# Two-layer encoder trunk on one Trainium2 core: other places for the short steps of seven-product pairs, and one weight sum moved from VectorE to an adding DMA

## What is computed

```python
h = rms_norm(x, mixer_norm_w)
# layer 0: q,k,v,u,g = split(h @ w_in); windowed attention beside gMLP gating
# layer 1: q,k,v = h @ w_qkv; stick-breaking attention
x = x + mixed @ w_out
h = rms_norm(x, ffn_norm_w)
x = x + (silu(h @ w_gate) * (h @ w_up)) @ w_down     # hidden width 5632
```

## Time and profile before

| | before |
|---|---|
| median of 3 runs | 2050.72 us (2050.27 to 2052.87) |
| the profiled execution | 2051.17 us, span 2049.4 us |
| PE busy | 2033.7 us, 99% |
| DVE busy | 1661.7 us, 81% |
| ACT busy | 1087.5 us, 53% |
| POOL busy | 162.7 us, 8% |
| DMA, mean | 221 GB/s |
| steps, matmuls of them | 846, 8724 |

### The profile page before, as it was taken

How to read it: one execution, slowest core, us unless ns; L and a number is a source line. 1 busy time by engine, 2 the same in 40 slices (tenths; PEclk the granted TensorE clock), 3 DMA queues, 4 the chain that set the end, 5 groups by cost and what they waited for, 6 DMA issues and landing times.

```text
span 2049.4 us, 23323 instructions
## 1 busy us (share of the span) xinstructions
PE 2033.7 (99%) x9176; PEld 1675.6 (82%) x9176; DVE 1661.7 (81%) x1859; ACT 1087.5 (53%) x1250; POOL 162.7 (8%) x271
## 2 busy tenths in 40 slices
PE   9999999999999999999999999999999999999999
PEld 8878878888888888888888888878888888888887
DVE  7777898888788887887666777888888788887986
ACT  6565555555445554555555455555554455544453
POOL 1010110010001000011111110110100001000010
PEclk9999999999999999999999999999999999999999
DMA  9665666566665666668767877676566666666664
GB/s 329 216 216 184 219 228 231 200 216 226 207 225 199 216 222 219 211 205 271 248 211 245 266 236 214 219 239 212 205 219 219 220 205 206 232 220 210 208 210 174
DMA packets 216431, 453.72 MB, mean 221 GB/s; under 512 B 10545, under 2 KB 10561, under 8 KB 216065
## 3 DMA queue, kind: packets, MB, share of 16 engines
q1 hardware_dynamic: 197600, 392.72, 56.1%
q0 software_dynamic: 18304, 57.37, 9.3%
q10 hardware_dynamic: 416, 2.13, 0.3%
HBM read 422.82 MB, written 29.36 MB: 221 GB/s over the span
## 4 chain that ended last, share of the span: by engine, by line
PE 60%; issue 29%; DMA 7%; DVE 2%; POOL 2%; ACT 0%; SPq 0%; POOLq 0%; DVEq 0%
PE acc L1483 17%; PE acc L1489 17%; PE acc L1484 17%; DMA spread<-blocks 3%; DMA blocks<-folded 3%; POOL spread L643 2%; PE turn_zb L1531 1%; PE turn_zb L1528 1%; PE turn_zb L1527 1%; PE acc L1531 1%; PE acc L1528 1%; PE acc L1527 1%; DVE w_lo L970 1%; DMA raw<-in_w_in 1%; DVE tsum L990 0%
## 5 line engine op out<-in xcount | busy, mean ns | idle before, releaser
L717 ACT ACTIVATE w_hi<-raw 128x1024 fp32r<-128x1024 f32 x710 | 742.4, 1056 | 494.5 <-PE acc L1489 479.2
L970 DVE TENSOR_TENSOR w_lo<-raw,w_hi 128x1024 fp32r<-128x1024 f32 x710 | 854.2, 1220 | 157.3 <-ACT w_hi L717 154.8
L1483 PE MATMUL acc<-w_hi,xT_hi 128*128 128x512 f32 x1664 | 649.9, 391 | 0.7 <-ACT w_hi L717 0.7
L1484 PE MATMUL acc<-w_hi,xT_lo 128*128 128x512 f32 x1664 | 647.7, 389 | 0.0
L1489 PE MATMUL acc<-w_lo,xT_hi 128*128 128x512 f32 x1664 | 444.9, 389 | 0.0
L1483 PEld LDWEIGHTS acc<-w_hi,xT_hi 128*128 128x128 f32 x1664 | 312.3, 188 | 67.9 <-issue 1.3
L1489 PEld LDWEIGHTS acc<-w_lo,xT_hi 128*128 128x128 f32 x1664 | 312.3, 188 | 65.1
L1484 PEld LDWEIGHTS acc<-w_hi,xT_lo 128*128 128x128 f32 x1664 | 312.4, 188 | 64.7
L717 ACT ACTIVATE w_hi<-tsum 128x1024 fp32r<-128x1024 f32 x136 | 144.5, 1062 | 303.0 <-DVE tsum L990 286.5
L1483 PE MATMUL acc<-w_hi,m_hi 128*128 128x512 f32 x764 | 297.9, 390 | 0.0
L1484 PE MATMUL acc<-w_hi,m_lo 128*128 128x512 f32 x764 | 297.3, 389 | 0.0
(11 more groups left out here) (222 smaller groups left out, 1676.8 us busy)
## 6 DMA issues: line engine op xcount, KB each, us to landing
raw<-in_w_gate SPq DMA_DIRECT2D x88, 1024.0 KB, 5.3
raw<-in_w_up SPq DMA_DIRECT2D x88, 1024.0 KB, 5.2
raw<-in_w_down SPq DMA_DIRECT2D x88, 1024.0 KB, 5.3
raw<-in_w_qkv SPq DMA_DIRECT2D x48, 1024.0 KB, 6.7
raw<-in_w_out SPq DMA_DIRECT2D x32, 1024.0 KB, 5.2
raw<-in_w_in SPq DMA_DIRECT2D x26, 1024.0 KB, 6.4
blocks<-folded POOLq DMA_DIRECT2D x42, 512.0 KB, 3.2
spread<-blocks POOLq DMA_DIRECT2D x168, 128.0 KB, 2.9
```

Source lines behind the costliest of these rows:

```text
L717: nc.scalar.activation(w_hi[:, h.slot, :, :], source(h), ACTF.Copy).then_inc(hi_ready, 1)
L970: nc.vector.tensor_tensor(w_lo[:, h.slot, :, :], source(h), f32(w_hi[:, h.slot, :, :]), ALU.subtract).then_inc(lo_ready, 1)
L1483: nc.tensor.matmul(dst, hi[:, h.k0 + k, at], wh, start=h.opens and k == 0, stop=False)
L1484: nc.tensor.matmul(dst, lo[:, h.k0 + k, at], wh, start=False, stop=False)
```

## The change

1. **Opening.** The order becomes A4 A6 B4 B6 A8 A10 B8 B10, then the seven short steps (outer P corner R outer Q W), then A12 A14 B12 B14. P, R and W are made ahead of steps 8, 10 and 13. The units are loaded in the new order.
2. **12-tile pairs.** A4 A6 B4 B6, then the seven short steps, then A8 A10 B8 B10.
3. **All other pairs.** The order is A4 A6 outer P B4 corner B6 R A8 Q outer W, and then as before. P, R and W are made ahead of steps 2, 6 and 10.
4. **Q's sum.** DVE no longer makes it. POOL issues a transfer from SBUF to SBUF, `raw[even] += raw[odd]` on chunk b's first unit (512 KB are added to 512 KB), as soon as the pair's P is made. ACT waits `q_added` before it rounds Q's weights, which it now reads from `raw`. That slot stays taken until Q's `w_lo` is made. POOL issues it between bounces, by step numbers (`FOLD_AT`).
5. **Wide corrections.** Pairs of VectorE instructions on 512 columns become one on 1024: the last two of `corrections`, the two of `corrected`, and the two that read PSUM in `leave` of gate and of up. A wide one waits for both row halves.

The core of the diff:

```diff
-SUMS = "PQRW"
-SUM_AT = {2: "P", 4: "Q", 7: "R", 10: "W"}
+SUMS = "PRW"
+SUM_AT = {2: "P", 6: "R", 10: "W"}
...
-    front = [A(4), A(6), ("outer", a, 0), ("P", -1, 0), B(4), ("Q", -1, 0), B(6), ("corner", b, 0), ("R", -1, 0)]
+    front = [A(4), A(6), ("outer", a, 0), ("P", -1, 0), B(4), ("corner", b, 0), B(6), ("R", -1, 0), A(8), ("Q", -1, 0), ("outer", a, 2), ("W", a, 0)]
     sums = dict(SUM_AT)
+    short = [("outer", a, 0), ("P", -1, 0), ("corner", b, 0), ("R", -1, 0), ("outer", a, 2), ("Q", -1, 0), ("W", a, 0)]
     if order == "opening":
-        sums = {2: "P", 4: "Q", 7: "R", 9: "W"}
-        steps = (front[:6] + [B(6), ("corner", b, 0), ("R", -1, 0), ("outer", a, 2), ("W", a, 0), A(8), A(10), B(8), B(10), A(12), A(14), B(12), B(14)])
-        units = [(a, 4), (b, 0), (a, 0), (b, 4), (a, 8), (b, 8), (a, 12), (b, 12)]
+        sums = {8: "P", 10: "R", 13: "W"}
+        steps = [A(4), A(6), B(4), B(6), A(8), A(10), B(8), B(10)] + short + [A(12), A(14), B(12), B(14)]
+        units = [(a, 4), (b, 4), (a, 8), (b, 8), (a, 0), (b, 0), (a, 12), (b, 12)]
     elif order == "together" and tiles == 12:
-        sums = {2: "P", 4: "Q", 7: "R", 9: "W"}
-        steps = front + [("outer", a, 2), ("W", a, 0), A(8), A(10), B(8), B(10)]
-        units = [(a, 4), (b, 0), (a, 0), (b, 4), (a, 8), (b, 8)]
+        sums = {4: "P", 6: "R", 9: "W"}
+        steps = [A(4), A(6), B(4), B(6)] + short + [A(8), A(10), B(8), B(10)]
+        units = [(a, 4), (b, 4), (a, 0), (b, 0), (a, 8), (b, 8)]
...
+            def add_q(pair):
+
+                slot = pair.it.unit_of(pair.b, 0) % RING
+                pool.wait_ge(sum_made, len(SUMS) * pair.n + 1)
+                pool.dma_start(raw[:, slot, 0::2, :], raw[:, slot, 1::2, :], accum_op=ALU.add).then_inc(q_added, 16)
...
             for F in range(len(FOLDS)):
                 if F == qk0 + 8:
                     bounce_weights(3)
+                for pair in PAIRS:
+                    if (FOLD_AT[F - 1] if F else 0) < pair.q_sum_at <= FOLD_AT[F]:
+                        add_q(pair)
                 bounce(F)
...
+                elif h.kind == "Q":
+                    act.wait_ge(q_added, 16 * h.pair.n + 16)
...
-                nc.vector.tensor_tensor(corr[:, 2, :], product[5], corr[:, 2, :], ALU.subtract)
-                nc.vector.tensor_tensor(corr[:, 3, :], product[5], corr[:, 1, :], ALU.subtract).then_inc(corr_made, 1)
+                nc.vector.tensor_tensor(corr[:, 2:4, :], product[5].unsqueeze(1).to_broadcast([P, TT, CH]), corr[:, 2:0:-1, :],
+                                        ALU.subtract).then_inc(corr_made, 1)
```

More of the change, by code:

```diff
@@ L108, in __init__ @@
         self.steps, self.units, sums = seven_steps(a, a + 1, tiles, order)
+        self.q_sum_at = it.base + first + min(sums)
         self.sums = {first + s: form for s, form in sums.items()}
@@ L166, in __init__ @@
         self.unit0 = unit0
-        self.halves = [Half(base + s, s, c, k, self.unit_of(of[s].a if c < 0 else c, k), kind, of[s]) for s, (kind, c, k) in enumerate(steps)]
+        homes = [c if c >= 0 else of[s].b if kind == "Q" else of[s].a for s, (kind, c, k) in enumerate(steps)]
+        self.halves = [Half(base + s, s, c, k, self.unit_of(homes[s], k), kind, of[s]) for s, (kind, c, k) in enumerate(steps)]
         for c in range(ph.chunks):
@@ L188, in release @@
         if k == 0 and self.pair_of(c):
-            last = max(last, max(t for t, form in self.pair_of(c).sums.items() if form in ("PQR" if c % 2 else "PW")))
+            last = max(last, max(t for t, form in self.pair_of(c).sums.items() if form in ("PR" if c % 2 else "PW")))
+            if c % 2:
+                last = max(last, max(h.s for h in self.halves if h.kind == "Q" and h.pair is self.pair_of(c)))
         return self.base + last
@@ L276, with group_start @@
             for c in ([1] if it.ph.name == "up" else range(2) if it.ph.name == "qkv" else range(it.ph.chunks))])
+GROUP0 = 22
+def group_start(g):
+    return GROUP0 + 7 * g
+FOLD_AT = ([group_start(g) + 6 + AHEAD for g in range(A_KV)]
+           + [it.base + it.fold_at(c) + AHEAD for it in ITERATIONS if it.ph.folds and it.ph.n
+              for c in ([1] if it.ph.name == "up" else [c for c in range(3) if QKV[it.i][c][0] != "v"] if it.ph.name == "qkv" else range(it.ph.chunks))])
 def splits(F):
@@ L514, in source @@
             if h.kind in SUMS:
-                return tsum[:, int(h.kind == "Q"), :, :]
+                return tsum[:, 0, :, :]
+            if h.kind == "Q":
+                return raw[:, h.raw_slot, 0::2, :]
             if h.kind == "corner":
@@ L669, in _ @@
                     bounce_weights(weights_follow[F])
+            for pair in PAIRS:
+                if pair.q_sum_at > FOLD_AT[-1]:
+                    add_q(pair)
             base = 2 * (D // CH) * (RESIDUALS - 1)
@@ L981, in weight_sum @@
                     out_to, a, b = tsum[:, 0, :, :], raw[:, gate % RING, even, :], first
[L982 to L983 removed]
                 elif form == "R":
[L985 removed]
+                    dve.wait_ge(sum_made, len(SUMS) * n + 1)
                     out_to, a, b = tsum[:, 0, :, :], tsum[:, 0, :, :], second
                 else:
[L988 removed]
+                    dve.wait_ge(sum_made, len(SUMS) * n + 2)
                     out_to, a, b = tsum[:, 0, :, :], tsum[:, 0, :, :], raw[:, gate % RING, odd, :]
@@ L1058, in corrected @@
                 dve.wait_ge(corr_made, pair.n + 1)
-                for tt in range(TT):
-                    xs = x_sb[:, tt, c * CH:(c + 1) * CH]
-                    nc.vector.tensor_tensor(xs, xs, corr[:, 2 * (c % 2) + tt, :], ALU.add).then_inc(x_corrected, 1)
+                xs = x_sb[:, :, c * CH:(c + 1) * CH]
+                nc.vector.tensor_tensor(xs, xs, corr[:, 2 * (c % 2):2 * (c % 2) + TT, :], ALU.add).then_inc(x_corrected, TT)
             def evacuate(it, c, dst, const=None):
@@ L1147, in leave @@
                     if c == 0:
-                        for tt in range(TT):
-                            dve.wait_ge(products_done, 2 * it.last_half(0) + tt + 1)
-                            nc.vector.tensor_tensor(hid[:, tt, :], acc[:, it.pair(0), tt, :], corr[:, tt, :], ALU.add).then_inc(acc_read, 1)
+                        dve.wait_ge(products_done, 2 * it.last_half(0) + TT)
+                        nc.vector.tensor_tensor(hid[:, :, :], acc[:, it.pair(0), :, :], corr[:, 0:TT, :], ALU.add).then_inc(acc_read, TT)
                         return
-                    for tt in range(TT):
-                        dve.wait_ge(products_done, 2 * it.last_half(1) + tt + 1)
-                        nc.vector.tensor_tensor(corr[:, 2 + tt, :], acc[:, it.pair(1), tt, :], corr[:, 2 + tt, :], ALU.add).then_inc(acc_read, 1)
+                    dve.wait_ge(products_done, 2 * it.last_half(1) + TT)
+                    nc.vector.tensor_tensor(corr[:, TT:, :], acc[:, it.pair(1), :, :], corr[:, TT:, :], ALU.add).then_inc(acc_read, TT)
                     dve.wait_ge(silu_done, ph.up0 + i + 1)
```

14 lines of the change are left out of this document (4 added, 10 removed).

## The result

The changed kernel takes **2063.17 us**, median of 4 runs (2061.86 to 2063.89), against 2051.28 us for the kernel before in the same session (4 runs, 2050.27 to 2052.87). The ratio is 1.0056, 95% interval 1.0042 to 1.0070: slower, by 11.9 us where 4.1 were forecast. The profiled execution took 2063.52 us, span 2061.7 us, 12.3 us longer than the span before.

A forecast was written before the change was run, and what follows sets the result against it. PE, busy 99% of the span, was taken as the bound. Openings +0.3, 12-tile pairs +2.3 and clock +1.5 gave +4.1 us, from 2050.7 to 2054.8 us; own range 2051 to 2060, wide range 2046 to 2064.

The forecast's parts named there:

- The gap at A8: In the openings: PE stands still 5.5 us at A8, now step 4, until chunk 2 of the stationary operand is ready.
- the two sums that leave: In the opening: DVE no longer makes sums P and Q before `var`, so the chain to `xT_lo` moves forward 2.27 us.
- rival 2: Openings win: chunk 2 comes sooner, PE waits 1.9 us at A8, -3.4 us per opening, total 2042.6; chance 0.16.
- Q in the openings: At Q in each opening: DVE's `w_lo` comes 0.5 us after PE wants it.
- The clock: PE's clock may fall to half speed after the openings' gaps; at most 3.0 us lost per opening, +1.5 taken.
- an even chance for each gap: The clock falls or holds with even chance in each opening's gap; 1.5 us was charged once.
- rival 4: Both clocks fall in full in the openings: +0.3 + 2.3 + 6.0, total 2059.3; no separate chance, within the forecast's range.
- The adding transfer: POOL's transfer for Q's sum takes 5.25 us, with 3.5 as lower and 11.0 as upper bound.
- The 12-tile pairs: Waits at A8 (0.77 us) and B8 (1.15), together 1.9 against 0.78 before: +1.15 each, +2.3 in all.
- The other 30 pairs: Outside openings and 12-tile pairs: transfer and saved DVE work hidden behind PE, costed at nothing.
- 1 (the clock holds): Rival, all even: the clock holds and the transfer takes 3.5 to 5 us, total 2049.7 to 2052.5; chance 0.22.
- 3 (a transfer over 9 us): Rival, slow adding transfer: +8 to +14 us at the 12-tile pairs, 2072 us at an 11 us transfer; chance 0.12.

The follow-up runs named there:

- early2: The changed kernel with chunk 2 of the stationary operand taken on ACT and DVE three steps earlier in the output phase: 2045.99 us, ratio 0.9968.
- fill2: The changed kernel with 24 warm-up products on PE ahead of its wait for chunk 2 at A8 in both openings: 2060.73 us, ratio 1.0045.
- dve_q: The changed kernel with Q's sum back on DVE and no adding transfer, new orders and wide corrections kept: 2059.25 us, ratio 1.0040.
- narrow: The changed kernel with all wide corrections split again into 512-column instructions: 2062.39 us, ratio 1.0047.
- before_early: The kernel before the change with only chunk 2 taken three steps earlier: 2052.28 us, ratio 1.0005.

## Why the prediction was right, and where it was not

The verdict (slower, with 2063.17 inside 2046 to 2064) was right, the forecast time 8.4 us too low. The measured time lies above the forecast's own range, 2051 to 2060, and 0.8 us from the edge of the wide one, and the loss is nearly three times the +4.1 that was added up. That sum lay on the line between no change and slower, with 0.45 against 0.40, so there was some luck in the verdict; what made it come out clear is that every term of the sum was larger than forecast. The places where PE would wait were right. By its steps:

- **The gap at A8**, 5.5 us: 5.74 and, in the second opening, 5.92. The reckoning by the two sums that leave (2.27 us; 2.28 measured) held. What it said of the cause was wrong in one word: the chain doesn't *hang on* the norm's scale. Chunk 2 only stood behind it in program order, as early2 shows, and rival 2 ("chunk 2 comes sooner") was one edit away; its gap of 1.9 us and its -3.4 per opening were too cautious, since early2 has no gap and -5.3.
- **Q in the openings**, 0.5 us late: 0.53 in both. With the gaps the orders alone gave 5.74 + 5.92 + 2 x 0.53 = 12.7 us where 2 x 5.84 = 11.7 were lost before: +1.0, and +0.3 was forecast.
- **The clock**, +1.5 us: the term that was mis-sized. It fell in both gaps, and in each PE was already at work for 5.57 and 3.99 us of the low stretch, half of which is lost: 2.8 + 2.0 = **4.8 us**; fill2, without it, gives 4.9 (2.4 in each, so the sums agree better than the openings one by one). The step that failed is "an even chance for each gap" and half of the loss; rival 4's price of 3.0 each was nearer. An even chance in each of two gaps at 3.0 us would have been 3.0, and the prediction gives no reason for taking half of that, with the warm-up rows showing half speed after idling. The Trainium skill's rule ("TensorE: Matmul & The Clock Gate", What's actually happening), that the throttled state is the default and activity lifts it, charged both gaps, +3.0 as I had written it. The trace agrees with it: the clock fell in both gaps, at a price of 4.8 us and not 3.0.
- **The adding transfer**, 5.25 us: 5.33 in the 12-tile pair, 5.1 median to landing over 34. In the two openings it took 8.3 and 8.4 to landing, which Q came late enough to hide. The bytes' rate of the earlier trace rows held. The Trainium skill's fit ("DMA: Bandwidth & Descriptors", Anatomy of one DMA) had given an estimate of 4.4 us; the measurement decides.
- **The 12-tile pairs**, +1.15 each: +2.2 and +1.9. The mis-sized term is POOL's start and not the transfer: the bounce was issued at 913.86 in the old time (913.6 forecast), its first transfer took 4.25 us where I took 3.5 from one row, and so the adding transfer left at 920.4, not 919.4. Q's weights came 1.0 us later than reckoned, and PE, which I had on time at Q by a hair, lost 1.33 there. A8 and B8 (0.46 and 1.24) came near the 0.77 and 1.15. The row was a fair one, 3.2 us to landing where the median over the program was 3.2 too; it was the transfer that got slower at this place, in dve_q without any adding transfer too, and the prediction had no term for that. (The median of the whole program rises to 4.2 mostly for the other reason, the adding transfer ahead of the bounce in the ordinary iterations.) The wide `corr` took 0.62 us from the fold, not 0.3.
- **The other 30 pairs**, nothing: +1.4 us over 20 iterations, 0.07 each. No wait for `raw<-raw` shows there. narrow gives 0.84 of it back; dve_q gives back none. What makes the rest, 0.1 us in one iteration of each phase, wasn't settled.
- **Rivals**: 1 (the clock holds) and 3 (a transfer over 9 us) are excluded. The result is rival 4 with a larger 12-tile term: 1.0 + 4.8 + 4.1 + 1.4 = 11.3 us, and 1.1 from the last stretch of qkv. Whether that last 1.1 is the change's is open. The stretch took 70.0 us in both profiled executions of the old order (before, before_early), and 70.0 to 71.6 in the twelve of new ones, 71.1 or more in four of them. The first stretch of qkv took 65.3 to 70.0 us, 66.0 and 70.0 in the old order, so there the spread is not the change's.

## What to carry to other kernels

When an order of steps is made for one engine's benefit, look up what each moved step needs, and then on which engine and behind what the maker of it stands: an operand may be late by its place in a queue and not by its data, and moving it three steps (early2) was worth more than the whole change cost. The part of an edit that is sound can be hidden by the part that isn't; run each alone. And a gap of 5.7 us on PE cost up to 2.8 us more than itself: count the clock's price in every such gap.
